# Norm ahead of the experts reduced to its weights, with merge, output product and first queries by column halves

## The reference, cut to what matters

```python
def rms_norm_2(x, g):
    y = xf * lax.rsqrt(jnp.mean(xf * xf, axis=-1, keepdims=True) + RMS_EPS)
    return (y * g)

merged = jax.nn.sigmoid(g_a) * ya + jax.nn.sigmoid(g_b) * yb
h = h + merged @ w_out

xt = rms_norm_2(h, norm_ffn_g)
qh = (xt @ w_peer_q).reshape(T, 8, 2, 128)
s = jnp.einsum('thpd,hpnd->thpn', qh, sub_keys)
sv, si = lax.top_k(s, 16)
# per head: 16 x 16 sums of the two halves, the best 16 of them, softmax -> gates
# per token: 8 heads x 16 experts
hval = jnp.einsum('cd,chkd->chk', xt, expert_u[ic])
a = gates * jax.nn.gelu(hval, approximate=False)
out = jnp.einsum('chk,chkd->cd', a, expert_v[ic])
```

## Time and profile before

| | |
|---|---|
| median of 3 runs | 1472.91 us |
| span of the profiled execution, first to last instruction | 1467.3 us |
| the profiled execution's own device time | not given apart; the median lies 5.6 us above the span |
| busy: TensorE / VectorE / ScalarE / POOL | 83% / 64% / 27% / 26% of the span |
| DMA | 484.31 MB, mean 330 GB/s; of them 268.45 MB gathered experts |
| chain that ended last | PE 45%, DMA 28%, VectorE 19%, issue 4%, ScalarE 3% |
| granted TensorE clock | 0.941 of full speed |

### The profile page before, as it was taken

How to read it: one execution, slowest core, us unless ns; L and a number is a source line. 1 busy time by engine, 2 the same in 40 slices (tenths; PEclk the granted TensorE clock), 3 DMA queues, 4 the chain that set the end, 5 groups by cost and what they waited for, 6 DMA issues and landing times.

```text
span 1467.3 us, 14350 instructions
## 1 busy us (share of the span) xinstructions
PE 1211.4 (83%) x4968; PEld 748.5 (51%) x4968; DVE 942.2 (64%) x2039; ACT 397.3 (27%) x1051; POOL 374.9 (26%) x285
## 2 busy tenths in 40 slices
PE   4989999999999999888787377668589887787776
PEld 3875655664767775487553265333473333232322
DVE  6288877973210231175866799996788776776654
ACT  2242111131101222122201223333234333333323
POOL 0001211201000000022533243432358444444420
PEclk9999999999999999999989699988799999999999
DMA  9733434465896667479999999999999999999996
GB/s 396 270 122 129 140 129 176 173 229 229 293 358 280 239 235 245 177 321 424 423 424 423 423 422 421 425 421 422 384 400 421 420 421 420 421 420 421 420 421 265
DMA packets 56376, 484.31 MB, mean 330 GB/s; under 512 B 6512, under 2 KB 8816, under 8 KB 10224
## 3 DMA queue, kind: packets, MB, share of 16 engines
q0 software_dynamic: 36864, 268.45, 44.2%
q1 hardware_dynamic: 18288, 211.35, 36.9%
q10 hardware_dynamic: 1152, 3.59, 0.6%
HBM read 482.33 MB, written 1.05 MB: 329 GB/s over the span
## 4 chain that ended last, share of the span: by engine, by line
PE 45%; DMA 28%; DVE 19%; issue 4%; ACT 3%; POOL 0%; DVEq 0%; SPq 0%; ACTq 0%
PE ps L517 23%; DMA ring<-in_euv,arena 16%; DMA arena<-in_euv,arena 7%; PE ps L613 6%; PE ps L980 6%; PE ps L904 5%; DVE xr L1910 4%; DMA ring<-in_w 3%; DVE arena L1886 3%; PE ps L1115 3%; DVE arena L1444 1%; DVE ring L1886 1%; DVE arena L1451 1%; DMA ring<-in_pq 1%; DVE arena L1180 1%
## 5 line engine op out<-in xcount | busy, mean ns | idle before, releaser
L2483 POOL DMA_INDIRECT arena<-in_euv,arena x161 | 206.1, 1280 | 575.2 <-DVE arena L1839 302.0
L517 PE MATMUL ps<-arena,ring 128*128 128x128 f32 (+1 forms) x1664 | 235.2, 305 | 28.8 <-DMA ring<-in_qkv 5.8
L517 PEld LDWEIGHTS ps<-arena,ring 128*128 128x128 f32 x1664 | 223.9, 204 | 44.4 <-issue 9.8
L1886 DVE CUSTOM_DVE_ANT_0 arena<-arena 128x1024 f32<-128x1024 f32 x161 | 195.5, 1223 | 69.9 <-DMA arena<-in_euv,arena 64.9
L517 PE MATMUL ps<-arena 128*128 128x128 f32 (+3 forms) x1276 | 178.9, 295 | 35.9 <-ACT arena L1999 23.0
L1115 PE MATMUL ps<-arena 128*128 128x512 f32 x356 | 173.5, 634 | 38.9 <-ACT arena L2355 38.5
L517 PEld LDWEIGHTS ps<-arena 128*128 128x128 f32 x1276 | 161.2, 194 | 65.5 <-issue 59.2
L2379 ACT ACTIVATE arena<-arena 128x2 f32<-128x2 f32 x127 | 25.7, 203 | 451.2 <-DVE arena L1886 450.7
L1115 PEld LDWEIGHTS ps<-arena 128*128 128x128 f32 x356 | 69.4, 201 | 139.7 <-issue 79.1
L980 PE MATMUL ps<-ring,arena 128*128 128x512 f32 x240 | 115.5, 639 | 25.0 <-DMA ring<-in_w 25.0
L1115 PE MATMUL ps<-ring,arena 128*128 128x512 f32 x216 | 103.7, 620 | 33.8 <-ACT arena L2355 33.8
(11 more groups left out here) (345 smaller groups left out, 1299.7 us busy)
## 6 DMA issues: line engine op xcount, KB each, us to landing
ring<-in_w SPq DMA_DIRECT2D x24, 2048.0 KB, 11.0
ring<-in_qkv SPq DMA_DIRECT2D x9, 2048.0 KB, 12.2
ring<-in_ada SPq DMA_DIRECT2D x8, 2048.0 KB, 7.9
ring<-in_gates SPq DMA_DIRECT2D x8, 2048.0 KB, 8.0
arena<-in_w SPq DMA_DIRECT2D x6, 2048.0 KB, 11.1
ring<-in_g SPq DMA_DIRECT2D x6, 2048.0 KB, 9.7
ring<-in_pq SPq DMA_DIRECT2D x6, 2048.0 KB, 12.2
ring<-in_wp SPq DMA_DIRECT2D x5, 2048.0 KB, 8.9
```

The lines of the kernel that those rows point to most:

```text
L517: ins = te.matmul(o, l, r, start=(i == 0), stop=(i == len(pairs) - 1))
L1886: ins = v.tensor_tensor_reduce(out=x, in0=x, in1=xn[:, tt, :], scale=1.0, scalar=0.0, op0=ALU.mult, op1=ALU.add, accum_out=hv[:, n % 16:n ...
L2483: gp.indirect_dma_start(slots[i], None, A["euv"], bass.IndirectOffsetOnAxis(ap=idx[:, n // 16 % 4, e % 16:e % 16 + 1].bitcast(U32), axis=0 ...
```

## The change

`late_units` has new units: `yT`, `wout` and `e` go by column halves (for `wout` the second number is the half of the product's depth), and the last two `ahead` halves of tile 0 stand behind `choose` 0. The norm's pass over the row goes; in its place each half of `xn` is `xr` times the weights, taken as soon as that half is summed. The factor is made beside it (`row_scale`) and multiplied in where ScalarE evacuates the scores, and as the scale of gelu. The first two query products of tile 0 do their first half of the depth before the second half of `xn` is transposed. ScalarE and VectorE exchange the halves that they copy. The costs and `ON_VECTOR` entries of these units change, and with them the places of tile 1's units. The same holds for tile 1, without the split query products.

```diff
-                gate(3, 1), branch(1, 0), branch(1, 1), (("yT",), 3), (("wout", 0), 10), (("wout", 1), 10),
-                (("e", 0), 10), *ahead[2:2 if tt else 3], (("e", 1), 4), *ahead[3:3 if tt else 4], (("pq", 0), 11))
+                gate(3, 1), branch(1, 0), branch(1, 1), (("yT", 0), 2), (("wout", 0, 0), 5), (("yT", 1), 2),
+                (("wout", 1, 0), 5), (("wout", 0, 1), 5), (("wout", 1, 1), 5), (("e", 0), 3), (("e", 1), 3),
+                (("pq", 0), 11))
     if tt == 0:
         yield ("choose", 0), 0
+        yield from ahead[2:4]
...
-             ("e", 0): 36, ("e", 1): 7, ("yT",): 7, ("wout",): 7, ("soft",): 4, ("forget",): 6}
+             ("e", 1): 13, ("yT", 1): 7, ("wout", 0, 1): 14, ("wout", 1, 1): 14, ("soft",): 4, ("forget",): 6}
```

On TensorE:

```diff
+            def first_half_of(name, c):
+
+                w = weights("pq", 0, 0)
+                if c == 0:
+                    te.wait_ge(*loaded("pq", 0, 0))
+                o = take(name, "main")
+                te.wait_ge(*empty("eT0.0"))
+                for k in range(4):
+                    te.matmul(o[:, 0:128], w[:, k * 512 + c * 128:k * 512 + c * 128 + 128], hL[0][:, k, :],
+                              start=(k == 0), stop=False)
...
-                queries(take("qp0.0a", "main"), 0, 0).then_inc(*fill("qp0.0a"))
-                queries(take("qp0.0", "main"), 1, 0).then_inc(*fill("qp0.0"))
+                rest_of("qp0.0a", 0)
+                rest_of("qp0.0", 1)
                 scored("sc0.0a", 0, 1)
...
                 elif what == "yT":
-                    te.wait_ge(sig("merged2"), 2 * tt + 2)
-                    rows_T(mg, f"yT{tt}")
+                    te.wait_ge(sig("merged2"), 2 * tt + i + 1)
+                    rows_T(mg, f"yT{tt}", halves=(i,))
                 elif what == "wout":
-                    if i == 0:
-                        te.wait_ge(*empty(f"yT{tt}.0"))
-                        te.wait_ge(*empty(f"yT{tt}.1"))
-                    for half in range(2):
-                        half_of(f"wz{tt}.{i}", ("wout", i, tt), tt, half)
-                elif what == "e" and i == 1:
-                    te.wait_ge(sig("xn"), NORMED[f"e{tt}"])
-                    rows_T(xn[:, tt, :], f"eT{tt}")
+                    te.wait_ge(*empty(f"yT{tt}.{half}"))
+                    half_of(f"wz{tt}.{i}", ("wout", i, tt), tt, half)
+                elif what == "e":
+                    te.wait_ge(sig("e_gained"), 2 * tt + i + 1)
+                    rows_T(xn[:, tt, :], f"eT{tt}", halves=(i,))
+                    if tt == 0:
+                        first_half_of("qp0.0" if i else "qp0.0a", i)
```

On VectorE:

```diff
                     emptied(v.tensor_tensor(xs, xs, psum(name)[:], ALU.add), name)
-                elif what == "e" and i == 0:
-                    v.wait_ge(sig("l_fg2"), 16 * tt + 16)
-                    norm(tt, 66, gt[:, 0, :])
-                elif what == "e":
-                    rows_T(tt, f"eT{tt}")
+                    after()
+                    tell(v.tensor_tensor(xn[:, tt, c], xs, gt[:, 0, c], ALU.mult), "e_gained")
+                elif what == "e" and i == 1:
+                    s_ = small[:, 66 + 8 * tt:74 + 8 * tt]
+                    norms[0] += 1
+                    v.wait_ge(sig("squares"), norms[0])
+                    tell(v.tensor_scalar(s_[:, 2:3], s_[:, 0:1], s_[:, 1:2], 1.0 / D, ALU.add, ALU.mult),
+                         "mean_square")
+                    rows_T(tt, f"eT{tt}", g=1)
+                    v.wait_ge(sig("root"), norms[0])
+                    tell(v.reciprocal(row_scale[tt], s_[:, 3:4]), "row_scale")
```

On ScalarE:

```diff
+            def scored(name, tt, j, n):
+
+                sc.wait_ge(sig("row_scale"), tt + 1)
+                sc.wait_ge(*full(name))
+                emptied(sc.mul(f4(scr[tt][:, j:j + n, :]), psum(name)[:, 0:128 * n], row_scale[tt]), name)
...
+                elif what == "wout" and i == 0 and half == 1:
+                    sum_squares(tt, 0)
                 elif what == "e" and i == 0:
+                    rows_T(tt, f"eT{tt}", g=0)
+                    tell(sum_squares(tt, 1), "squares")
+                elif what == "e":
                     root(tt, 66)
...
-                done(sc.activation(gl, hv[:, n % 16:n % 16 + GROUP], ACT.Gelu))
+                done(sc.activation(gl, hv[:, n % 16:n % 16 + GROUP], ACT.Gelu, scale=row_scale[PICKS[n][0]]))
```

73 lines of the change are left out of this document (43 added, 30 removed).

## The result

The changed kernel takes 1463.61 us (median of 6 runs, 1460.35 to 1467.8), the kernel before in the same comparison 1472.39 (1469.1 to 1474.8). The ratio is 0.9931, with a 95% interval of 0.9916 to 0.9947: 10 us, with an interval of 8 to 12.

What follows compares the result with a forecast made beforehand. From about 642 to 1452 us the DMA transfers were taken to bound the kernel. 10.6 - 4.2 + 1.0 = 7.4 us off 1472.9 gave 1465.5 us, range 1460.0 to 1470.4.

Steps and rivals of the forecast that it cites:

- Part 1: Chain of tile 0 from merge to first top-k: first gather at 629.6 us, 10.6 us earlier.
- The cover that I named for the root: Tile 0's norm: factor ready at 618.7 us, scores want it at 620.4; without that cover, 1.3 us cost.
- The 1.8 us that I put on the clock: Tile 0's output product: share of the 10.6 us that rests on TensorE running at full clock after a shorter wait.
- The scale of gelu: The factor in ScalarE's gelu instruction: claimed to cost nothing, hidden by the matmuls or ScalarE's idleness.
- Part 2: Behind the first gathers: TensorE's releases come only 2.9 us earlier, so idle DMA gives back 4.2 us.
- The two new waits: Fourth gather waits for `ahead` 6, no loss; eighth for `pq` 1, 2 us late, covered by gathers in flight.
- no loss: Loads of `pq` by SyncE, from 614.4 us instead of 617.6, claimed to be through by 630.5 at no cost.
- Part 3: Tile 1: VectorE waits less, wait for the output product under 1 us; 1.0 us gained from the DMA hole.
- The whole shift: Rival for the gathers' start: "issue" gaps go away, 10.6 plus 0 to 2.7 us gained, 1459.6 to 1462.3; chance 0.20.
- Only TensorE's 2.9: Rival: slot and weight releases by TensorE decide, the end moves by 2.9 us alone, 1470.0; chance 0.13.
- The strewn units: Rival in tile 1: units falling up to a group later hold VectorE up, kernel slower, 1476.4; chance 0.05.
- The clock rival: Rival in tile 0: the clock drop stays or moves to the queries, 1.8 us less gain, 1467.3; chance 0.12.

Runs made afterwards that it cites:

- order_as_before: Changed kernel with two unit costs raised so that tile 1's strewn units fall where they fell in the kernel before; 1463.69 us.
- halves_only: Changed kernel with the factor multiplied into the rows again and tile 0's `ahead` units placed as in the kernel before; only the column halves stay; 1470.38 us.
- ahead_first: Changed kernel with the two moved `ahead` units of tile 0 put back ahead of the first query product; 1470.43 us.
- factor_on_rows: Changed kernel with the factor multiplied into the rows again ahead of the transposes, halves and moved `ahead` units kept; 1467.91 us.
- before_ahead_moved: Kernel before with only the two `ahead` units of tile 0 moved behind the first query product; ratio 1.0000.
- vector_late_50: Changed kernel with 50 more one-column reciprocals on VectorE in tile 1 behind the row factor, about 10 us of work; 1468.67 us.
- ahead_last: Changed kernel with tile 0's `ahead` units moved behind all its query products, and the slots they need used last; 1463.47 us.
- last_and_order: Changed kernel with tile 0's `ahead` units behind all its query products and tile 1's units strewn as in the kernel before; 1463.57 us.
- gather_later: Changed kernel with POOL's first gather waiting for the whole first choice of tile 0 instead of its first maximum; 1468.59 us.

## Why the prediction was right, and where its terms were not

**The bound.** Right: from the first gather to the last landing the transfers set the time. G to D is 816.4 to 819.0 us in thirteen of the fourteen profiles of the table, whatever TensorE and VectorE do in them, and 822.5 with the hole that I made.

**Part 1, first gather 10.6 us earlier.** Measured 11.0. With the 7.4 us by which this profile is late, the second halves of the first queries were due at 625.65 (measured 625.13) and the first scores at VectorE at 628.2 (627.87). The cover that I named for the root held: the reciprocal was done at 625.3 us and the scores came at 627.5. The 1.8 us that I put on the clock are the weak place: in the two profiles compared they are there, but the kernel before doesn't always lose them. By the rule of the Trainium skill that I cited (TensorE: Matmul & The Clock Gate, "What's actually happening") another wait could catch the drop, and one did: that ahead of the rest of the product with `pq` 1. Waits of 4.43 and 5.04 us were each followed by matmuls at half rate here. The scale of gelu, which I put at nothing, has a price, but a hidden one (last section).

**Part 2, 4.2 us given back.** Measured 2.6. The mechanism was right, an idle place at the tenth gather, but mis-sized. TensorE's release came 5.4 us earlier, not 2.9. I had kept the "issue" gaps in the product with `pq` 2, where the rows showed them. They came in that with `pq` 1, 4.1 us of them with the slow clock (11.4 us for its 64 matmuls against the 7.31 of the other products), and `pq` 2 and 3 took 7.31 each. The two new waits were there; the eighth gather stood 6.28 us instead of 2, under the cover of seven gathers in flight. The query weights were still landing when the gathers began (DMA share 0.86 in 635 to 640, where it was 0.00), which I had put aside with "no loss": about 0.5 MB that had been moved ahead of G now come behind it (the transfers that start behind G hold 340.2 MB in after and 339.7 before). order_as_before has those bytes and no slow clock, and 817.0 us: the bytes cost about 0.6 us, the slow clock 2.

**Part 3, 1.0 us gained in tile 1.** Measured 0. VectorE's waits did not shrink to under 1 us; its timeline of after in tile 1, which answers to the earlier trace rows:

```profile
1031.16 0.69 DVE L1827 TENSOR_TENSOR xr<-xr,ps 128x512 f32<-128x512 f32 x1 [1.38 <-PE ps L910]
...
1034.53 0.69 DVE L1827 TENSOR_TENSOR xr<-xr,ps 128x512 f32<-128x512 f32 x1 [1.95 <-PE ps L910]
...
1042.78 0.21 DVE L1834 TENSOR_SCALAR small<-small 128x1 f32<-128x1 f32 x1 [1.97 <-ACT arena L2271]
...
1044.69 0.16 DVE L1838 RECIPROCAL small<-small 128x1 f32<-128x1 f32 x1 [1.10 <-ACT small L2049]
```

3.3 us for the product where there were 5.66, and 3.1 for the norm where there were 2.26. The hole closed all the same, and that was worth nothing: halves_only, ahead_first and factor_on_rows have no hole at 1050 to 1070 and 816.4 to 816.7 us, before and before_ahead_moved have it (2.6 and 1.2 us) and 816.4 and 816.7. The step that failed is the one that took the idle time of the transfers for time: of a longer hole, 5.6 us in vector_late_50, 2 were free too.

**The sum.** 10.6 - 4.2 + 1.0 = 7.4 was forecast, 11.0 - 2.6 + 0 = 8.4 found, and the ratio says 10 with an interval of 8 to 12. The errors in parts 2 and 3 went against each other, and that the sum came so near is in part luck: the draws of the clock, 1.7 us in before and 2 in after, are as large as the terms that they sit in.

**The rivals.** The whole shift did not come through in the profiles, 8.4 us of 11.0. But the premise of that rival was right and mine was wrong: the "issue" gaps sit just behind the start of the gathers, wherever TensorE is, and in after the product with `pq` 2 ran free of them. Without the slow clock, in the profiles of order_as_before, ahead_last and last_and_order, 10.3 to 10.4 us of the shift come through, and by the times (8 to 12 us) the whole shift is not excluded for the changed kernel itself. "Only TensorE's 2.9" fell with the release itself. The strewn units hold nobody up (ahead_last against last_and_order). The clock rival was real as a mechanism but is a draw of each execution on both sides. The median I had set 5.6 us above the span; in nearly all profiles here a run takes 1.3 to 1.5 us more than its span, so the profiled execution of before was itself a short one, of about 1468.7 us (an estimate). That does not touch the difference.

## What to carry to other kernels

Where one queue of transfers fills the rest of the program, count from the transfer that opens it: find the chain ahead of it, and measure every change from a common instant just before that chain, since what lies ahead can move by more than the change is worth. Parts of such a chain are not additive: work that fills a wait and the wait itself have to go together, and tried one at a time each looked worth 1 us of the 5. Before pricing a hole in the transfers, see how evenly the DMA engines end: where one ends late, part of a hole can come free. And an instant at which the clock drops in one profile may be a draw: look at a second execution before a forecast rests on it.

## What the hardware showed that I had not expected

- **The DMA engines do not end together.** In after the share is 0.74 in 1440 to 1450 us and 0.03 in the next ten, while dot products still wait for landings until 1455.68: 0.03 of 16 engines over 10 us is 4.8 us of one engine. In windows of 1 us the share stays near 0.06, one of 16, from 1450 on, and the trace holds just one packet in flight for 5.7 us ahead of D; before it is 1.9 us. So it goes in all fourteen profiles: 1.9 to 2.4 us in the three with a hole of over 1 us (before, before_ahead_moved, vector_late_50), 4.5 to 6.5 in the others. In vector_late_50 all are full to 1450. That one engine lags fits the free hole there (2 us of 5.6) and that of before, as it could go on while the others stood; that it did so, and what makes it lag, wasn't tried.
- **The clock fell after TensorE's waits, but not each time.** After waits of 4.43, 5.04 and 5.54 us the next matmuls ran at half rate, with a granted clock of 0.51, 0.53 and 0.52. After two short waits (about 1.6 and 0.7 us) the same product took 8.79 us in one kernel and 7.11 in another, with the same instructions up to there.
- **The "issue" gaps of TensorE go with the transfers' start**, not with a product: they follow the first gather by 9.6 us before and 7.6 after (gaps from 649.9 us with G at 640.26; from 644.3 with G at 636.69), and by 7.5 to 9.6 in every profile but that of gather_later, which has the "remote" waits there instead. Why is open.
- **A factor per row in ScalarE's instruction is not free.** The gelu over 128x2 takes 294 ns with it and 203 without, 12 us over the kernel, hidden by ScalarE's idle time. In factor_on_rows, which takes the factor out of it again, it is back at 203. The groups of before and of after:

```profile
L2379 ACT ACTIVATE arena<-arena 128x2 f32<-128x2 f32 x127 | 25.7, 203 | 451.2 <-DVE arena L1886 450.7
```
```profile
L2425 ACT ACTIVATE arena<-arena,small 128x2 f32<-128x2 f32 x127 | 37.4, 294 | 433.6 <-DVE arena L1916 433.4
```
